# One weight stream in three passes per half, parameters on the weight queue, and three moved steps

## The reference

```python
# first block
h = rms_norm(x, norm_g)
q, kv, g, z_a, uv, z_b, merge = split(h @ w_in)            # 2048 -> 10800 columns
o_a = nsa_attention(q, kv, g, ...) * silu(z_a)
o_b = spatial_gating(uv, ...) * silu(z_b)
x = x + (sig(merge_a) * (o_a @ w_up_a) + sig(merge_b) * (o_b @ w_up_b)) @ w_out
x = x + sigmoid(x @ w_ple_gate) * (p @ w_ple)
x = rms_norm(x, final_g)
# second block, on 16 meta tokens + 256 tokens = 272
h = concat(meta, x)
u = rmsnorm(h)                                             # even layer
z_a, xs, B, C, dt_f, dt_b, z_b, val, gate = split(u @ e_w_in)
y_a = rmsnorm(ssd(silu(conv5(xs, B, C)), dt) * silu(z_a))  # both directions
y_b = silu(layernorm(conv31(val * sigmoid(gate)))) * silu(z_b)
h = h + concat(y_a, y_b) @ e_w_out
u = rmsnorm(h)                                             # odd layer
q, k, v, z = split(u @ o_w_in)
h = h + (neighbourhood_attention(q, k, v, rpb) * silu(z)) @ o_w_out
return rmsnorm(h)[:, 16:]
```

## Time and profile before

| what | value |
|---|---|
| median of 3 runs | 2268.86 us (2267.65 to 2269.37) |
| the profiled execution | 2268.41 us, its span 2266.7 us |
| granted TensorE clock, mean | 0.997 |
| PE busy | 2235.3 us, 99% of the span |
| DVE, ACT, POOL busy | 68%, 48%, 18% |
| chain of work that ended last | PE 89%, DVE 8%, others 1% each |
| PE waiting for other engines or transfers, summed | 22 us |

### The profile page before, as it was taken

The page is one execution under the profiler, slowest core; times in us unless marked ns, Lnnn a source line. Parts: engine busy times, 40 slices in busy tenths (PEclk is TensorE's granted clock), DMA queues, the critical chain, the costliest instruction groups (busy, mean ns, idle before and its releaser), DMA issues.

```text
span 2266.7 us, 43103 instructions
## 1 busy us (share of the span) xinstructions
PE 2235.3 (99%) x18446; PEld 2174.8 (96%) x18446; DVE 1547.3 (68%) x2611; ACT 1082.4 (48%) x1625; POOL 415.4 (18%) x340
## 2 busy tenths in 40 slices
PE   7999999999999999999999999999999999999998
PEld 7999999999999999999999988999999999999998
DVE  5556655664565567669899988898746447777554
ACT  4345555644544455343333666554535444444443
POOL 7010000000000000088777300570001001010000
PEclk9999999999999999999999999999999999999999
DMA  9665445656556555555555556565555545555652
GB/s 235 175 123 177 149 149 154 187 167 186 186 186 186 186 186 169 160 166 178 158 168 174 178 174 176 155 192 174 182 169 168 167 145 168 152 150 169 205 185 94
DMA packets 379119, 385.88 MB, mean 170 GB/s; under 512 B 14309, under 2 KB 372197, under 8 KB 378741
## 3 DMA queue, kind: packets, MB, share of 16 engines
q1 hardware_dynamic: 374288, 377.99, 54.5%
q0 software_dynamic: 2896, 3.76, 1.5%
q10 hardware_dynamic: 1744, 1.38, 0.2%
HBM read 380.72 MB, written 4.12 MB: 170 GB/s over the span
## 4 chain that ended last, share of the span: by engine, by line
PE 89%; DVE 8%; ACT 1%; issue 1%; DMA 1%; POOL 0%; SPq 0%; ACTq 0%; DVEq 0%
PE ps L448 27%; PE ps L450 26%; PE ps L449 26%; DVE ps L1784 2%; PE ps L2538 1%; DVE wlo L401 1%; PE ps L2358 1%; PE ps L2587 1%; PE ps L2375 1%; DMA raw<-in_w_in_dram 1%; PE ps L2607 1%; PE ps L2567 0%; PE ps L2394 0%; ACT whi L394 0%; DVE op_lo L525 0%
## 5 line engine op out<-in xcount | busy, mean ns | idle before, releaser
L448 PE MATMUL ps<-op_hi,whi 128*128 128x256 f32 (+1 forms) x5440 | 1569.5, 289 | 10.1 <-POOL wlo L401 4.5
L450 PE MATMUL ps<-op_hi,wlo 128*128 128x256 f32 (+1 forms) x5440 | 1551.3, 285 | 0.0
L449 PE MATMUL ps<-op_lo,whi 128*128 128x256 f32 (+1 forms) x5440 | 1548.3, 285 | 0.0
L394 ACT ACTIVATE whi<-raw 128x1024 fp32r<-128x1024 f32 (+1 forms) x688 | 722.6, 1055 | 885.8 <-PE ps L450 861.0
L448 PEld LDWEIGHTS ps<-op_hi,whi 128*128 128x128 f32 x5440 | 1026.7, 189 | 28.3 <-issue 19.6
L450 PEld LDWEIGHTS ps<-op_hi,wlo 128*128 128x128 f32 x5440 | 1027.8, 189 | 0.0
L449 PEld LDWEIGHTS ps<-op_lo,whi 128*128 128x128 f32 x5440 | 1025.6, 189 | 0.4 <-issue 0.2
L401 DVE TENSOR_TENSOR wlo<-raw,whi 128x1024 fp32r<-128x1024 f32 x554 | 668.0, 1222 | 449.1 <-ACT whi L394 448.1
L401 POOL TENSOR_TENSOR wlo<-raw,whi 128x1024 fp32r<-128x1024 f32 x134 | 326.8, 2447 | 1068.5 <-ACT whi L394 1068.2
L1784 DVE SCALAR_TENSOR_TENSOR ps<-arena,param_cols,ps 128x257 f32<-128x257 f32 (+6 forms) x448 | 183.3, 488 | 0.4
L1475 DVE SCALAR_TENSOR_TENSOR arena<-arena,nslopes,ps 128x128 f32<-128x128 f32 (+1 forms) x64 | 23.7, 412 | 50.0 <-PE ps L2358 49.1
(11 more groups left out here) (396 smaller groups left out, 1454.8 us busy)
## 6 DMA issues: line engine op xcount, KB each, us to landing
raw<-in_e_w_in_dram SPq DMA_DIRECT2D x96, 1024.0 KB, 5.4
raw<-in_w_in_dram SPq DMA_DIRECT2D x84, 1024.0 KB, 5.2
raw<-in_o_w_in_dram SPq DMA_DIRECT2D x64, 1024.0 KB, 5.9
raw<-in_e_w_out_dram SPq DMA_DIRECT2D x32, 1024.0 KB, 5.7
raw<-in_w_out_dram SPq DMA_DIRECT2D x16, 1024.0 KB, 5.6
raw<-in_w_ple_gate_dram SPq DMA_DIRECT2D x16, 1024.0 KB, 5.7
raw<-in_o_w_out_dram SPq DMA_DIRECT2D x16, 1024.0 KB, 5.7
arena<-cum_rows SPq DMA_DIRECT2D x16, 544.0 KB, 6.2
```

Of the source, the lines that this page charges most:

```text
L394: nc.scalar.activation(half_view(whi[c % 2], c, n), half_view(raw[c % RING], c, n), ACT.Copy).then_inc(hi_ready, 1)
L448: nc.tensor.matmul(o, wh, xh, start=(i % cpp == 0 and k == 0), stop=False)
L449: nc.tensor.matmul(o, wh, xl, start=False, stop=False)
L450: mm = nc.tensor.matmul(o, wl, xh, start=False, stop=(i % cpp == cpp - 1 and k == 7))
```

## The change

The three products of a half are issued as three passes of eight matmuls instead of eight triples. The first pass needs `whi` (`hi_ready`) and the high groups of the operand (for h1 still the low ones), the second the low groups, the third `wlo`. The 13 parameter transfers go to SP's queue, issued behind chunk 1 of kvc, so ahead of chunks 2 and 3. The square root of the conformer norm moves from i == 5 to 6 on ACT, variance and reciprocal from 5 and 6 to 6 and 7 on DVE, the total of squares on PE from after chunk 7 to after chunk 8. `conv31(3, 3)` moves behind the operand's low parts and the last pair of gg. At the end of z2 DVE's order is changed.

```diff
--- before.py
+++ after.py
@@ -433,21 +433,29 @@
             b = 2 * ((s.p0 + j) % 2)
             if n == 0 and i % cpp == 0 and s.p0 + j >= 2:
                 pe.wait_ge(acc_free, s.p0 + j - 1)
-            lo_wait(pe, c, n)
-            for k in range(8):
-                t = tile0 + 8 * (i % cpp) + k
+            o = ps[:, b + n, 0:NT]
+
+            def group_wait(sem, t):
                 if need is not None and n == 0 and j == 0:
                     g0, groups = SPL[need]
                     per = 8 * cpp // groups
                     if (t - tile0) % per == 0:
-                        pe.wait_ge(ml_ready, g0 + (t - tile0) // per + 1)
-                wh = hi8[c % 2][:, k, n * P:(n + 1) * P]
-                wl = lo8[c % 2][:, k, n * P:(n + 1) * P]
-                xh, xl = MH[:, t, off:off + NT], ML[:, t, off:off + NT]
-                o = ps[:, b + n, 0:NT]
-                nc.tensor.matmul(o, wh, xh, start=(i % cpp == 0 and k == 0), stop=False)
-                nc.tensor.matmul(o, wh, xl, start=False, stop=False)
-                mm = nc.tensor.matmul(o, wl, xh, start=False, stop=(i % cpp == cpp - 1 and k == 7))
+                        pe.wait_ge(sem, g0 + (t - tile0) // per + 1)
+
+            pe.wait_ge(hi_ready, 2 * c + n + 1)
+            for k in range(8):
+                t = tile0 + 8 * (i % cpp) + k
+                group_wait(ml_ready if need == "h1" else mh_ready, t)
+                nc.tensor.matmul(o, hi8[c % 2][:, k, n * P:(n + 1) * P], MH[:, t, off:off + NT], start=(i % cpp == 0 and k == 0), stop=False)
+            for k in range(8):
+                t = tile0 + 8 * (i % cpp) + k
+                group_wait(ml_ready, t)
+                nc.tensor.matmul(o, hi8[c % 2][:, k, n * P:(n + 1) * P], ML[:, t, off:off + NT], start=False, stop=False)
+            lo_wait(pe, c, n)
+            for k in range(8):
+                t = tile0 + 8 * (i % cpp) + k
+                mm = nc.tensor.matmul(o, lo8[c % 2][:, k, n * P:(n + 1) * P], MH[:, t, off:off + NT],
+                                      start=False, stop=(i % cpp == cpp - 1 and k == 7))
             mm.then_inc(half_done, 1)
 
         def stream_pe(pe, name, NT=S1, off=0, tile0=0, need=None, lo=0, hi=None):
@@ -553,7 +561,24 @@
             for part in range(4):
                 tt, cols = part // 2, slice(1024 * (part % 2), 1024 * (part % 2) + 1024)
                 nc.sync.dma_start(xnat[:, tt, cols], A["x"][0, P * tt:P * tt + P, cols]).then_inc(S(f"x_landed_{part}"), 16)
-            for n in ("kvc", "qa", "qb", "kvs"):
+            def load_params(i):
+                if i != 1:
+                    return
+                rows = [("e_norm_g_2", R_ENORM), ("e_ssd_norm_g_2", R_SSD),
+                        ("o_norm_g_2", R_ONORM), ("e_ln_g_2", R_LNG), ("e_ln_b_2", R_LNB), ("e_dw_b_2", R_DWB)]
+                srcs = [(A[n], r, 1) for n, r in rows]
+                srcs += [(A["final_g"].rearrange("(a n) -> a n", a=1), R_FINAL, 1),
+                         (A["e_dw_w_2"][0], R_DW, K31),
+                         (A["e_conv_w_2"][0].rearrange("k (h n) -> (k h) n", h=2), R_CW, 2 * K5),
+                         (A["e_conv_b_2"].rearrange("a (h n) -> (a h) n", h=2), R_CB, 2),
+                         (A["meta_tokens_2"], R_META, META)]
+                for src, r, n in srcs:
+                    nc.sync.dma_start(PR[r:r + n, :], src).then_inc(S("params_landed"), 16)
+                nc.sync.dma_start(PR[R_LNV:R_LNV + 1, 0:BW], A["ln_v_g"]).then_inc(S("params_landed"), 16)
+                nc.sync.dma_start(PR[R_LNV:R_LNV + 1, BW:D], A["ln_v_b"]).then_inc(S("params_landed"), 16)
+
+            load_stream(sp_eng, "kvc", between=load_params)
+            for n in ("qa", "qb", "kvs"):
                 load_stream(sp_eng, n)
             s = ST["gate"]
             load_chunk(sp_eng, s, 0, raw[s.c0 % RING][:, 0:DT * 48].rearrange("p (t n) -> p t n", t=DT),
@@ -652,18 +677,6 @@
             diag(ident, ALU.is_equal, 1)
             diag(triF, ALU.is_ge, 1)
             diag(triB, ALU.is_ge, -1)
-            rows = [("e_norm_g_2", R_ENORM), ("e_ssd_norm_g_2", R_SSD),
-                    ("o_norm_g_2", R_ONORM), ("e_ln_g_2", R_LNG), ("e_ln_b_2", R_LNB), ("e_dw_b_2", R_DWB)]
-            srcs = [(A[n], r, 1) for n, r in rows]
-            srcs += [(A["final_g"].rearrange("(a n) -> a n", a=1), R_FINAL, 1),
-                     (A["e_dw_w_2"][0], R_DW, K31),
-                     (A["e_conv_w_2"][0].rearrange("k (h n) -> (k h) n", h=2), R_CW, 2 * K5),
-                     (A["e_conv_b_2"].rearrange("a (h n) -> (a h) n", h=2), R_CB, 2),
-                     (A["meta_tokens_2"], R_META, META)]
-            for src, r, n in srcs:
-                nc.gpsimd.dma_start(PR[r:r + n, :], src).then_inc(S("params_landed"), 16)
-            nc.gpsimd.dma_start(PR[R_LNV:R_LNV + 1, 0:BW], A["ln_v_g"]).then_inc(S("params_landed"), 16)
-            nc.gpsimd.dma_start(PR[R_LNV:R_LNV + 1, BW:D], A["ln_v_b"]).then_inc(S("params_landed"), 16)
             halves(pool, "pool", 0)
             halves(pool, "pool", 1)
             side("kvc")
@@ -1190,7 +1203,7 @@
                         if g >= 2:
                             act.wait_ge(S("cf_added"), 2 * g - 3)
                         nc.scalar.activation(SQX[:, g % 2, :, :], op(GU, T2)(g), ACT.Square).then_inc(norm_sq, 1)
-                if i == 5:
+                if i == 6:
                     act.wait_ge(norm_ms, cf + 1)
                     nc.scalar.activation(rstd[:, :], ms[:, :], ACT.Sqrt).then_inc(norm_rt, 1)
                 if 8 <= i < 12:
@@ -1809,7 +1822,7 @@
                     dt_bias()
                 if i == 1:
                     softplus()
-                for k in {2: (0,), 3: (1,), 4: (2, 3), 5: (4,), 6: (5, 6), 7: (7,), 8: (8, 9)}.get(i, (i + 1,) if 9 <= i < 15 else ()):
+                for k in {2: (0,), 3: (1,), 4: (2, 3), 5: (4,), 6: (5, 6), 7: (7,), 8: (8, 9)}.get(i, (i + 1,) if 9 <= i < 14 else ()):
                     if k % 4 == 0:
                         dve.wait_ge(S("tmp_used"), TMPC["gg"] + k // 8 + 1)
                     conv31(k // 4, k % 4)
@@ -1827,6 +1840,7 @@
             h2s_lo(2)
             h2s_lo(3)
             gg_times(7)
+            conv31(3, 3)
             dve.wait_ge(S("tmp_used"), TMPC["gg"] + 8)
             for d in range(2):
                 dve.wait_ge(S("cum_psum"), d + 1)
@@ -1971,13 +1985,12 @@
                     conv31(12 + i // 4, i % 4)
             ya_lo(0)
             ya_lo(1)
-            split_lo(dve, "dve", s.end + 1, 0)
             pair_wait(dve, s, 7)
             z2_times(7, (s.p0 + 7) % 2)
+            sum_pair(dve, 0, 5, T2)
             ya_lo(2)
             ya_lo(3)
-            sum_pair(dve, 0, 5, T2)
-            split_lo(dve, "dve", s.end + 1, 1)
+            halves(dve, "dve", s.end + 1)
             sum_pair(dve, 0, 6, T2)
             sum_pair(dve, 0, 7, T2)
             conv31(15, 2)
@@ -2030,10 +2043,10 @@
                 if i == 4:
                     cf_half(2)
                     cf_half(3)
-                if i == 5:
+                if i == 6:
                     dve.wait_ge(S("cf_squares"), 1)
                     V.tensor_scalar(ms[:, :], ps[:, 4, 0:T2], 1.0 / D, EPS2, ALU.mult, ALU.add).then_inc(norm_ms, 1)
-                if i == 6:
+                if i == 7:
                     dve.wait_ge(norm_rt, cf + 1)
                     v.do(V.reciprocal(rstd[:, :], rstd[:, :]))
                     v.sync()
@@ -2550,7 +2563,7 @@
                 if i == 2:
                     pe.wait_ge(S("conv31_state"), 2)
                     T.matmul(ps[:, 5, 0:T2], ones[:, :], CSUM[:, :], start=True, stop=True).then_inc(S("cf_sum"), 1)
-                if i == 7:
+                if i == 8:
                     pe.wait_ge(S("cf_added"), 7)
                     for t in range(2):
                         mm = T.matmul(ps[:, 4, 0:T2], ones[:, :], SQA[:, t, :], start=(t == 0), stop=(t == 1))
```

## The result

The changed kernel takes 2253.88 us (median of 3 runs, 2253.54 to 2254.02) against 2268.86: ratio 0.9935, interval 0.9921 to 0.9949.

A forecast was written before the change was run, and what follows sets the result against it. PE, busy 2235.3 of 2266.7 us with one stream of matmuls, was taken as the bound; the terms summed to -7.55 us, from 2268.4 profiled to 2260.9, forecast 2261.2 as the median, range 2257.0 to 2267.0.

The forecast's parts named there:

- Order of the passes: In all halves: no matmul added or removed, inputs due later, spacing unchanged; taken as 0, within 3 us either way.
- Rival B: Matmul spacing changes with the order: slower, 2277.5 us, chance 0.05; faster, to 2250, chance 0.03.
- The start: Kvc's first half: the 4.3 us wait turns into another wait with more matmuls behind it; taken as 0.
- 29 at the latest: At the start: chunk 2 lands by 29 us, 3 us to spare, so moving the parameters costs 0.
- Rival C: At the start: parameters hold the weight queue, chunk 2 lands near 40, total 2270.3 us; chance 0.08.
- 30.5: At the start: landing of chunk 2 in us if the 31-row transfer lies on one engine, still inside the cover.
- xs: At the start of xs: PE's wait for the low part of x and the lowered clock go, -3.8 us.
- oa: After z2's end: waits for low weights and the total of squares go, a later one comes; together -2.7 us.
- gg: In gg: PE's one wait for POOL's low weights goes, -0.45 us.
- the small ones: Waits in gv and v shrink by 0.1 us each, and the o3 share goes for -0.4 us.
- the conv sums' total: In oa: PE, come earlier at 1540.55, waits until 1541.45 for DVE's last conv piece.
- The moved conv piece: Behind gg's last pair: makes DVE's cum copies 2.2 to 3.0 us late under 3.3 cover; cost 0, at most 1.

The follow-up runs named there:

- e13: The changed kernel in the old order of triples, all three products high weights by high operand, both low parts left out; 2269.5 us (one run).
- e17: The changed kernel with each pass's tiles in the order 0 5 2 4 1 6 3 7, waiting for the operand's group before every tile; 2247.9 us (one run).

## Why the prediction was wrong

**Order of the passes: the step that failed.** The text says "giving up that neighbourhood costs nothing by these rows", "I take 0", and bounds the term at 3 us either way. It was -10.6. That term was taken at nothing, and it is the largest of the ledger. From equal counts of weight loads and matmuls I concluded that the distance doesn't depend on the order. The counts show only that each matmul loads; they say nothing of how long a load and a matmul lie apart. My own remark that rows 3 bound it badly was right, and the bound of 0.2 ns a matmul had no row behind it; 0.65 ns were measured. What the runs show in place of the 0: the order of the tiles sets the mean distance, 118.2 ns in triples for 117.6 in passes (256 columns), 126.0 for 125.4 (272). Rival B had the right scale (1 ns is 16.3 us) and gave the faster side 0.03. Its argument against itself, that the spacing is the same "whatever kind comes before", was a wrong reading. In the trace of the kernel before, with 256 columns, the second product starts 117.0 ns after the first, the third 119.1 after the second, the next triple 118.6 after the third (e13 shows that this goes with the place in the order and not with the kind). Its 23 places run from 116 to 121 ns with 256 columns and from 120 to 130 with 272, in one fixed pattern.

**The start.** "I take 0" for the first half was right: the second began at 24.98, then 25.10. Chunk 0 came at 12.9 as forecast, the low parts at 18.4 and 21.1. Wrong was "29 at the latest" for chunk 2: the 10.8 us of the parameters on POOL's queue were no bound for another queue, which gave the 31 rows to a single engine. Rival C was the mechanism, at a fifth of its price (+1.9 for +9). The Trainium skill's rule on the engines of a transfer, "DMA: Bandwidth & Descriptors", section "Why a DMA increments its semaphore by 16 and not by 1", holds here: share 0.06 for 6 us and more. My estimate from it, 30.5, was 3 us short. With the taps cut in 16 and 15 rows it is gone.

**xs, oa, gg, the small ones.** Right in place and size: -3.8 and -3.8; -2.7 and -2.8, with the conv sums' total late as named (0.84 for a forecast of 0.9); -0.45 and -0.45. The small ones brought 0.2 of the 0.6 forecast: gv and v gained nothing, since PE came earlier and waits there for the low operand all the same (0.6 and 0.5). The moved conv piece cost nothing, and DVE's splits kept up. Not seen was 0.7 at upa: its first pass outruns ACT's high parts there.

**The sizes of the repaired waits** hold only beside the passes: alone, without the other parts, the passes bring 5.9 us; the other parts alone bring nothing (2269.67 against 2268.62, within the noise). The forecast added them as if each stood by itself; that the waits came out right is owed to their being made together.

## What to carry to other kernels

Where PE is 99% busy, look at the distance between matmuls before the waits: 0.65 ns over 16,320 of them were worth more than the waits repaired, and permuting the tiles inside an accumulation, which adds no instruction, another 7 us. Which order is best no run here tells beforehand; that of e17 was found by trial. Cut a transfer on a hardware queue into row counts that many engines can share. A wait repaired on PE moves every deadline after it, so undo the parts singly to see which still pay.

## What the runs showed of the hardware

- The mean distance of fp32r matmuls hangs on the order of the tiles: 116.9 to 118.3 ns with 256 columns, 125.2 to 126.0 with 272, at full clock and with the same number of instructions.
- A 31-row load of 248 KB on SP's queue ran 6 us and more at 25 to 27 GB/s with a DMA share of 0.06, the next chunk behind it.
- A wait of 2 to 3 us in the middle of the stream cost about double: 2.1 us at xs cost 4.6, 3.2 us at oa 6.2. Behind both the granted clock was at its half level (1.2 GHz), at which the matmuls lie 0.227 us apart with 272 columns (0.213 with 256). Behind the waits of 1.0 us at chunk 2 and 0.84 us at the conv sums, in the changed kernel, it stayed at full.
- An earlier start of matmuls can be taken back by the clock: 1.2 us earlier, and half clock for 6.8 instead of 3.4 us.
